# Gate matrices from two fp32r pieces, with one compare and one product for four tokens

## What is computed

```python
q = (t @ w_pq).reshape(T, PEER_HEADS, 2, PEER_HALF)
s = einsum('thpk,hpnk->thpn', q, sub_keys)
top_s, top_i = lax.top_k(s, PEER_TOPK)                       # 16 of 128 keys, twice per head
cand_s = top_s[:, :, 0, :, None] + top_s[:, :, 1, None, :]
best_s, best_pos = lax.top_k(cand_s.reshape(...), PEER_TOPK) # 16 of 256 pairs
gate = jax.nn.softmax(best_s, axis=-1)
act = gelu(einsum('td,thkd->thk', t, expert_down[experts]))
out = einsum('thk,thkd->td', gate * act, expert_up[experts])
```

## Time and profile before

| what | us |
|---|---|
| median of 3 runs | 3011.03 (3009.43 to 3012.24) |
| the profiled execution | 3016.37 |
| its span | 3014.6 |
| PE busy | 2911.4 |
| DVE busy | 2404.4 |
| ACT busy | 1478.6 |
| POOL busy | 691.7 |

### The profile page before, as it was taken

The page is one execution under the profiler, slowest core; times in us unless marked ns, Lnnn a source line. Parts: engine busy times, 40 slices in busy tenths (PEclk is TensorE's granted clock), DMA queues, the critical chain, the costliest instruction groups (busy, mean ns, idle before and its releaser), DMA issues. The chain is left out here.

```text
span 3014.6 us, 49268 instructions
## 1 busy us (share of the span) xinstructions
PE 2911.4 (97%) x19366; PEld 2671.4 (89%) x19366; DVE 2404.4 (80%) x4049; ACT 1478.6 (49%) x2443; POOL 691.7 (23%) x374
## 2 busy tenths in 40 slices
PE   7899999999999998999999999999899999999998
PEld 7798989879898987999999888888799999988887
DVE  5978998687899876898997677777599899656665
ACT  3453434445443444545665455554444666545554
POOL 0100000010000011797665000001289666300000
PEclk9999999999999998999999999999899999999999
DMA  6435555543555552454445777873245444555554
GB/s 221 154 138 204 198 200 190 199 168 133 187 198 209 189 193 92 170 182 156 141 141 189 242 262 260 290 272 118 105 166 184 141 140 141 175 182 194 191 195 161
DMA packets 125976, 547.96 MB, mean 182 GB/s; under 512 B 13715, under 2 KB 17972, under 8 KB 101300
## 3 DMA queue, kind: packets, MB, share of 16 engines
q1 hardware_dynamic: 124572, 542.73, 51.5%
q10 hardware_dynamic: 1176, 2.10, 0.4%
HBM read 538.48 MB, written 6.29 MB: 181 GB/s over the span
## 5 line engine op out<-in xcount | busy, mean ns | idle before, releaser
L2025 POOL TENSOR_TENSOR q_lo<-q_raw,q_hi 128x1024 fp32r<-128x1024 f32 x250 | 624.9, 2506 | 261.7 <-ACT q_hi L2135 261.4
L2044 PE MATMUL k_psN<-k_hhi,q_hi 128*128 128x256 f32 x2304 | 666.6, 289 | 0.7 <-ACT e_hv L2199 0.2
L2044 PE MATMUL k_psN<-k_hhi,q_lo 128*128 128x256 f32 x2304 | 652.9, 283 | 0.0
L2044 PE MATMUL k_psN<-k_hlo,q_hi 128*128 128x256 f32 x2304 | 652.7, 283 | 0.0
L2135 ACT ACTIVATE q_hi<-q_raw 128x1024 fp32r<-128x1024 f32 x538 | 565.3, 1051 | 6.6 <-DMA q_raw<-down 3.5
L2338 DVE TENSOR_TENSOR q_lo<-q_raw,q_hi 128x1024 fp32r<-128x1024 f32 x288 | 352.9, 1225 | 130.6 <-ACT q_hi L2135 130.0
L2044 PEld LDWEIGHTS k_psN<-k_hhi,q_hi 128*128 128x128 f32 x2304 | 443.0, 192 | 3.1 <-DVE k_hlo L2364 2.4
L2044 PEld LDWEIGHTS k_psN<-k_hlo,q_hi 128*128 128x128 f32 x2304 | 443.3, 192 | 0.0
L2044 PEld LDWEIGHTS k_psN<-k_hhi,q_lo 128*128 128x128 f32 x2304 | 442.4, 192 | 0.0
L752 DVE TENSOR_TENSOR k_wlo<-k_raw,k_whi 128x2048 fp32r<-128x2048 f32 x158 | 360.9, 2287 | 95.2 <-ACT k_whi L572 94.4
L572 ACT ACTIVATE k_whi<-k_raw 128x2048 fp32r<-128x2048 f32 x158 | 301.7, 1913 | 230.6 <-PE f_psA L424 99.6
(11 more groups left out here) (357 smaller groups left out, 5485.1 us busy)
## 6 DMA issues: line engine op xcount, KB each, us to landing
k_raw<-ws SPq DMA_DIRECT2D x180, 1024.0 KB, 4.8
q_raw<-down SPq DMA_DIRECT2D x288, 512.0 KB, 3.4
q_raw<-up SPq DMA_DIRECT2D x256, 512.0 KB, 4.0
k_x<-ada SPq DMA_DIRECT2D x48, 512.0 KB, 3.6
e_ada<-ada SPq DMA_DIRECT2D x48, 512.0 KB, 5.1
out<-k_x SPq DMA_DIRECT2D x3, 1024.0 KB, 3.9
k_x<-out SPq DMA_DIRECT2D x3, 1024.0 KB, 6.2
k_x<-x SPq DMA_DIRECT2D x2, 1024.0 KB, 6.0
```

The source lines that it names most:

```text
L2025: nc.gpsimd.tensor_tensor(lo[:, i % RING, :], raw[:, i % RING, :], hi[:, i % RING, :].bitcast(F32), ALU.subtract).then_inc(S["lo_pool"], 1)
L2044: last = nc.tensor.matmul(psD(n), w, h, start=kt == 0 and i == 0, stop=kt == KT - 1 and i == 2)
```

## The change

The gates are split into two fp32r pieces, `gT_hi` (rounded) and `gT_lo` (the difference). One DVE compare of 128x1024 for four tokens writes both one-hot matrices, for i1 and for i2 (`compared`). The rows of the first matrix are multiplied by the high piece in one 128x512 DVE product (`high_rows`), and by the low piece in four ScalarE activations of 128x128 with one scale per partition (`low_rows`). PE multiplies the one-hot matrix of i2 by both, in two fp32r matmuls per token, summed in PSUM. The buffers of a group are two deep instead of three, the ring B has 6 slots instead of 11. DVE's order in an iteration becomes `compared(g)`, `into_a(g-2)`, `high_rows(g)`, `gate_early(g-3)` (for g = 0 and 1 the high rows follow the compare at once). ScalarE's own rows, which needed no other engine, are gone; `low_rows` waits for the compare.

```diff
@@ -1857,10 +1857,10 @@
 ND = PQ + NE
 NU = ND + NE
 FIRST = 45
-SLOTS = 11
+SLOTS = 6
 GROUP = 4
 GROUPS = T // GROUP
-HOTS = 3
+HOTS = 2
 RING = 3
 
 INSIDE = GROUPS
@@ -1907,13 +1907,15 @@
     pb = arena(nc, env["X_at"], tag)
     B_at = pb.at[0]
     B = pb("e_b", [P, SLOTS, T])
-    i1T, i2T, gT = (pb("e_" + n, [P, T]) for n in ("i1T", "i2T", "gT"))
-    ngT = pb("e_ngT", [P, GROUPS])
+    iT = pb("e_iT", [P, 2, T])
+    gT_hi = pb("e_gThi", [P, T], F32R)
+    gT_lo = pb("e_gTlo", [P, T])
     iota = pb("e_iota", [P, P])
     hot_at = pb.at[0]
-    hot1 = pb("e_hot1", [P, HOTS, GROUP, NE])
-    hot2 = pb("e_hot2", [P, HOTS, GROUP, NE])
-    assert pb.at[0] == env["peer_at"]
+    hot = pb("e_hot", [P, HOTS, 2, GROUP, NE], F32R)
+    row_hi = pb("e_rhi", [P, HOTS, GROUP, NE], F32R)
+    row_lo = pb("e_rlo", [P, HOTS, GROUP, NE], F32R)
+    assert pb.at[0] <= env["peer_at"]
     raw, hi, lo = env["peer_ring"]
     A_at = pb.at[0] = env["ring_at"]
     A = pb("e_a", [P, NE, T])
@@ -1958,7 +1960,7 @@
         psN = env["psN"]
         ps = cx.enter_context(nc.psum_tensor("e_ps" + str(l), [P, 4, CH], F32))
         names = """in_const in_keys diag_ready half_done tile_diag hv_ready h_lo_ready norm_mm lo_pool lo_dve unit_done psd_read score_mm sc_copied
-            dve_step t_sub t_exp iv_ready picks_mm picks_copied hot1_ready hot2_ready hot1_act dist_ready neg_ready w_mm w_read_dve w_read_act
+            dve_step t_sub t_exp iv_ready picks_mm picks_copied hot_ready row_hi_ready row_lo_ready w_mm w_read_dve w_read_act
             weighted g_hi_ready g_lo_ready gate_mm gate_ready prod_done x_done out_x in_crow in_ada ada_done""".split()
         S = {n: cx.enter_context(nc.semaphore("e_" + n + str(l))) for n in names}
         raw_in = [Q["raw0"], Q["raw1"], Q["raw2"]]
@@ -2056,14 +2058,14 @@
 
                 def gates(g):
 
-                    pe.wait_ge(S["hot1_ready"], g + 1)
-                    pe.wait_ge(S["hot2_ready"], g + 1)
-                    pe.wait_ge(S["hot1_act"], g + 1)
+                    pe.wait_ge(S["row_hi_ready"], g + 1)
+                    pe.wait_ge(S["row_lo_ready"], g + 1)
                     if g >= 4:
                         pe.wait_ge(S["w_read_act"], g - 3)
                     for k in range(GROUP):
-                        last = nc.tensor.matmul(ps[:, g % 4, k * NE:(k + 1) * NE], hot2[:, g % HOTS, k, :], hot1[:, g % HOTS, k, :],
-                                                start=True, stop=True)
+                        for i, row in enumerate((row_hi, row_lo)):
+                            last = nc.tensor.matmul(ps[:, g % 4, k * NE:(k + 1) * NE], hot[:, g % HOTS, 1, k, :], row[:, g % HOTS, k, :],
+                                                    start=i == 0, stop=i == 1)
                     last.then_inc(S["w_mm"], 1)
 
                 def up(x):
@@ -2167,16 +2169,15 @@
                     act.wait_ge(S["score_mm"], h + 1)
                     nc.scalar.activation(sc[:, h, :, :].rearrange("p a n -> p (a n)"), psS(h), ACT.Copy).then_inc(S["sc_copied"], 1)
 
-                def gated_last(g):
-
-                    k = GROUP - 1
-                    t = g * GROUP + k
+                def low_rows(g):
+
                     if g >= HOTS:
                         act.wait_ge(S["w_mm"], g - HOTS + 1)
-                    row = hot1[:, g % HOTS, k, :]
-                    nc.scalar.activation(row, iota[:, :], ACT.Abs, bias=i1T[:, t:t + 1], scale=-1.0).then_inc(S["dist_ready"], 1)
-                    act.wait_ge(S["dist_ready"], g + 1)
-                    nc.scalar.activation(row, row, ACT.Relu, bias=gT[:, t:t + 1], scale=ngT[:, g:g + 1]).then_inc(S["hot1_act"], 1)
+                    act.wait_ge(S["hot_ready"], g + 1)
+                    for k in range(GROUP):
+                        t = g * GROUP + k
+                        ins = nc.scalar.activation(row_lo[:, g % HOTS, k, :], hot[:, g % HOTS, 0, k, :].bitcast(F32), ACT.Copy, scale=gT_lo[:, t:t + 1])
+                    ins.then_inc(S["row_lo_ready"], 1)
 
                 def to_a(g):
 
@@ -2207,17 +2208,15 @@
                         scores_out(n // 2 - 1)
                     head(n + RING)
                 act.wait_ge(S["picks_copied"], 3)
-                nc.scalar.activation(ngT[:, :], gT[:, :].rearrange("p (g k) -> p g k", k=GROUP)[:, :, GROUP - 1], ACT.Copy, scale=-1.0).then_inc(S["neg_ready"], 1)
-                act.wait_ge(S["neg_ready"], 1)
-                gated_last(0)
-                gated_last(1)
+                low_rows(0)
+                low_rows(1)
                 for g in range(GROUPS):
                     if g:
                         n = PQ + FIRST + g - 1
                         take(n)
                         head(n + RING)
                     if g + 2 < GROUPS:
-                        gated_last(g + 2)
+                        low_rows(g + 2)
                     to_a(g)
                 for n in range(PQ + FIRST + INSIDE - 1, ND):
                     take(n)
@@ -2303,18 +2302,19 @@
                     own.link(V.tensor_tensor(hots[:, :, :, :], hots[:, :, :, :], num, ALU.mult))
                     own.step(V.tensor_reduce(iv[:, 0:2, :, h * 16:(h + 1) * 16].rearrange("p k t s -> p (k t) s"), hots[:, :, :, :], AX.X, ALU.add))
 
-                def gated(g):
+                def compared(g):
 
                     if g >= HOTS:
                         dve.wait_ge(S["w_mm"], g - HOTS + 1)
-                    for k in range(GROUP - 1):
-                        t = g * GROUP + k
-                        ins = V.tensor_scalar(hot1[:, g % HOTS, k, :], iota[:, :], i1T[:, t:t + 1], gT[:, t:t + 1], ALU.is_equal, ALU.mult)
-                    ins.then_inc(S["hot1_ready"], 1)
-                    tokens = slice(g * GROUP, (g + 1) * GROUP)
-                    V.tensor_tensor(hot2[:, g % HOTS, :, :], iota[:, :].rearrange("p (a n) -> p a n", a=1).to_broadcast([P, GROUP, NE]),
-                                    i2T[:, tokens].rearrange("p (a n) -> p a n", n=1).to_broadcast([P, GROUP, NE]),
-                                    ALU.is_equal).then_inc(S["hot2_ready"], 1)
+                    numbers = iT[:, :, g * GROUP:(g + 1) * GROUP].rearrange("p a (k n) -> p a k n", n=1).to_broadcast([P, 2, GROUP, NE])
+                    places = iota[:, :].rearrange("p (a k n) -> p a k n", a=1, k=1).to_broadcast([P, 2, GROUP, NE])
+                    V.tensor_tensor(hot[:, g % HOTS, :, :, :], places, numbers, ALU.is_equal).then_inc(S["hot_ready"], 1)
+
+                def high_rows(g):
+
+                    dve.wait_ge(S["hot_ready"], g + 1)
+                    high = gT_hi[:, g * GROUP:(g + 1) * GROUP].bitcast(F32).rearrange("p (k n) -> p k n", n=1).to_broadcast([P, GROUP, NE])
+                    V.tensor_tensor(row_hi[:, g % HOTS, :, :], hot[:, g % HOTS, 0, :, :].bitcast(F32), high, ALU.mult).then_inc(S["row_hi_ready"], 1)
 
                 def into_a(g):
 
@@ -2375,18 +2375,25 @@
                 own.link(V.tensor_reduce(esum[:, :], e, AX.X, ALU.add))
                 own.link(V.reciprocal(esum[:, :], esum[:, :]))
                 V.tensor_tensor(e, e, esum[:, :].rearrange("p (a c) -> p a c", c=1).to_broadcast([P, 16, 16]), ALU.mult).then_inc(S["iv_ready"], 1)
-                for i, dst in enumerate((i1T, i2T, gT)):
-                    dve.wait_ge(S["picks_mm"], i + 1)
-                    V.tensor_copy(dst[:, :], ps[:, i, 0:T]).then_inc(S["picks_copied"], 1)
+                dve.wait_ge(S["picks_mm"], 2)
+                V.tensor_copy(iT[:, :, :], ps[:, 0:2, 0:T]).then_inc(S["picks_copied"], 1)
+                dve.wait_ge(S["picks_mm"], 3)
+                V.tensor_copy(gT_hi[:, :], ps[:, 2, 0:T]).then_inc(S["picks_copied"], 1)
+                dve.wait_ge(S["picks_copied"], 2)
+                V.tensor_tensor(gT_lo[:, :], ps[:, 2, 0:T], gT_hi[:, :].bitcast(F32), ALU.subtract).then_inc(S["picks_copied"], 1)
                 dve.wait_ge(S["picks_copied"], 3)
 
                 for g in range(GROUPS + 3):
                     if g < GROUPS:
-                        gated(g)
+                        compared(g)
+                        if g < HOTS:
+                            high_rows(g)
+                    if 2 <= g < GROUPS + 2:
+                        into_a(g - 2)
+                    if HOTS <= g < GROUPS:
+                        high_rows(g)
                     if g >= 3:
                         gate_early(g - 3)
-                    if 2 <= g < GROUPS + 2:
-                        into_a(g - 2)
                 for n in range(PQ + FIRST + INSIDE, ND):
                     weigh(n)
                     rest(n + RING)
```

## The result

| | before | after |
|---|---|---|
| median, us (4 runs each) | 3011.64 (3009.43 to 3012.44) | 3077.34 (3075.0 to 3080.63) |
| the profiled execution, us | 3016.37 | 3077.74 |
| its span, us | 3014.6 | 3076.0 |

The change makes the kernel slower: the ratio is 1.0219 with an interval of [1.0206, 1.0232]. That is 65.7 us between the medians and 61.4 us between the two profiled executions. Forecast was +54, 3065 us, with a range of 3038 to 3130.

The account below looks back on a forecast made before the run. PE bounds the kernel before; after the change DVE's and POOL's turns were to set the gate stage's pace. Turns 43, phase 14 and first gates -3 gave +54 us on 3011: 3065 us, range 3038 to 3130 us.

Parts of the forecast that it names:

- PE gains nothing: Gate products on PE: 8 fp32r records replace 8 at 0.112 to 0.120 us, losing at most 0.06 us a group.
- Rival 1: Gate products on PE: fp32r no cheaper than fp32 at 128 columns, 0.224 us each, 3121 us; chance 0.27.
- rival 3: Gate stage: DVE-POOL turns are no bound, PE decides; with records at 0.081 us, 2977 us; chance 0.09.
- The turn cycle of 4.02 to 4.27 us: Gate stage: DVE and POOL alternating take mean 4.15 us a group against PE's 3.77, 48 us in all.
- the lead: DVE starts each layer's gate stage 2.6 us ahead of PE; eating that up cuts the loss from 48 to 43 us.
- Rivals 3 and 4: Gate stage: turns are no bound; records cheaper than 0.112 us (chance 0.09), or at 0.112, 3008 to 3015 us (0.07).
- First gates -3 us: Start of the second layer's gates: two turns behind POOL replace four, shortening PE's wait by about 3 us.
- ScalarE and DMA hide: Gate stage: ScalarE's 2.7 us a group fits under 3.77 us; DMAs and their queue are untouched.
- The phase term of +14 us: Later 63 groups: in half, POOL precedes the compare and DVE's product into A lies bare, 32 x 0.45 us.
- A close finish goes to POOL: Gate stage: when a DVE compare and POOL's subtraction start nearly together, POOL gets its turn first.
- Rival 2: Gate stage: every POOL turn falls ahead of the compare, +97 us, 3108 us; chance 0.07.
- Fewer buffers are free but for the lead: Gate stage: two hot buffers only limit DVE's lead of 2.6 us; 6 slots of ring B cost nothing.

Follow-up runs that it names:

- E9: The changed kernel with DVE making POOL's low halves in the gate stage, each gate product cut into two of 64 columns: 3126.59 us.
- E3: The changed kernel with ScalarE's low rows of two tokens made in two halves each, six activations for four: 3056.84 us.
- E1: The changed kernel with POOL subtracting only the first 512 of 1024 columns for the gate stage's tiles: 3014.07 us.
- E2: The changed kernel with POOL's whole subtraction for the gate stage's tiles given to DVE: 3014.99 us.
- E12: The kernel before with a ring B of 6 slots in place of 11, keeping three hot buffers: 3012.28 us.
- E4: The changed kernel without the low piece of each fourth token, one activation and one gate product less per group: 3095.91 us.
- E11: The changed kernel with only DVE's new compare and product, in fp32, no low rows, three hot buffers, 5 slots of B: 3075.61 us.
- E7: The kernel before with the change's buffers alone, two hot buffers for three and 6 slots of B for 11: 3037.02 us.
- E6: The kernel before with POOL's subtraction for the gate stage's tiles given to DVE: 3009.72 us, ratio 0.9999.
- E8: The changed kernel with POOL's gate-stage subtraction on DVE, no low rows, and PE using the gates' high piece only: 2957.58 us.

## Why the prediction was right, and where it was off

Every step below is one of the prediction's own.

- **PE gains nothing: right.** Eight records at 0.112 us for eight. Rival 1 (0.224 us a record, 3121 us) falls by the rows at 1420 us, rival 3's cheaper record by the same rows and by E9. What the prediction held for rival 1, a fixed cost "that fp32 doesn't have", isn't in its rows: an fp32 record of 128 columns at 0.112 us is 0.059 us over 128 columns at 2.4 GHz (0.053 us), more than fp32r's 0.013.
- **The turn cycle of 4.02 to 4.27 us: right.** E3 shows it undisturbed, from 4.06 to 4.27, 4.22 in the mean of the last 25; the change has 4.04 in its first groups. The forecast sum of 43 us after the lead compares with E3's 41.6. That the price of one turn (3.35 us) was taken from another stage did no harm. Rivals 3 and 4, turns no bound, fall by E1 and E2.
- **First gates -3 us: not shown, the near match is luck.** In the two profiled executions the first gates come 1.3 and 1.5 us earlier, where 3 us were forecast for the second layer alone. But the wait of 4.44 us belongs to that one execution of before. E12, the kernel before with fewer slots of B and the same median, waits less:

```profile
2352.06 2.04 PE L2065 MATMUL e_ps<-e_hot,e_hot 128*128 128x128 f32 x8 [2.67 <-ACT e_hot L2179]
```

The changed kernel waits the same 2.67 us, for ScalarE's low rows. Against E12 its first gates are level in the first layer (1393.43 and 1393.45 us) and 0.8 us later in the second.
- **ScalarE and DMA hide: right as work, wrong as time.** ScalarE was never late for PE after the first group, but the moment at which it lets POOL go is worth 20 us either way (E3, E4).
- **The phase term of +14 us: the step that failed.** That the product into A lies bare once POOL comes ahead of the compare was right, the size not, and that POOL's turns would come in pairs was not foreseen. I put the release at 4.12 us, and it is 4.25 falling to 4.15; I priced a bare product at 0.45 us, and it is 4.68 - 4.22 = 0.46. What failed is the count: "half of the later 63 groups", 32. Once the crossing has come, every group to the end of the layer pays in the mean, 25 a layer, 50 in all: 23 us (22.4 by the whole stages). The groups there are 3.83 to 5.59 us apart, outside the 4.0 to 4.4 that the prediction named as its sign. "Half" was a guess where the numbers allowed a count, the cycle as it grows from group to group against the release.
- **A close finish goes to POOL: wrong as a rule.** At 1538.34 POOL is recorded 0.03 us ahead and the compare runs free; at 1546.68 it is 0.03 us ahead and the compare stands. The recorded starts don't tell who wins when they are 0.03 us apart. The Trainium skill (SBUF — State Buffer, "Who interferes with whom") lets whoever issues first hold the shared pair; starts this close, like those of the earlier trace rows, can neither confirm nor refute it.
- **Rival 2, every turn ahead of the compare (3108 us): not the change,** whose turns are behind it for 38 intervals. E4 comes near it with 3095.91 us, and its turns too come in pairs.
- **Fewer buffers are free but for the lead: right here, wrong in general.** For the changed order E11 bears it out in fp32 and without the low rows; with them no run has three hot buffers. For the old order two hot buffers cost 26 us (E7), with turns bunched in the same way, which I didn't see coming.
- **The carried offset.** The profiled execution of before lay 5.3 us over its median, that of after 0.4 us over. In profiled time I forecast 3070.4 and got 3077.74, off by 7.4: +8.4 for the phase, -1.4 for the turns, 0.4 for the rest. By the medians I am off by 12.3, and the other 4.9 us are this offset. It lies where the two layers' gates begin: E12's span is 5.8 us shorter than that of before, 1.3 and 2.3 us of it before the first gates and 1.5 and 0.7 in the first interval behind them. The prediction carried it over to a kernel that doesn't show it.

What stays open: no version was found that keeps both pieces of the gates and beats before; E1 leaves work out and E2 only draws level. The change with both pieces and three hot buffers was not run: by the sizes in the code they take more than the stage has for them. Why POOL's turns pair up, and stay paired, is read from timelines; no run changed that link alone. PE's 8 records and 24 matmuls hold the groups at 3.77 us with and without the change once POOL is out of the way (E2, E6), which makes a gain there unlikely unless products are left out, as in E8.

## What to carry to other kernels

When two engines take turns on something, count the turn-taking work of each per period (here 1.31 us became 1.94) and add the other's whole turn; if the sum passes the period of the engine that binds, the turns set the pace (here 4.0 to 4.3 us for 3.77), and fewer instructions don't help. Then compare the length of that cycle, group by group, with the delay at which the other engine is released: where they crossed here, overlap was lost until the end of the layer, and moving the release by 0.3 us, in one direction by adding work to ScalarE, was worth about 20 us either way. And before shortening a stall that the profile shows, ask whether anyone waits for it (E6: 25 us of DVE's time in a stretch of 230, nothing gained).

## What the runs showed of the hardware

- A gate product of 64 or 128 columns in fp32r costs 0.112 us in a stream (E9, the change), as does each of the two records of an fp32 product of 128 columns (before).
- DVE's compare of two repeated (broadcast) inputs, writing fp32r, takes turns with POOL as the product of the earlier trace rows does: 1.21 us free, 3.41 to 3.43 behind a subtraction.
- TensorE's granted clock fell after some of the new idle spells. In the changed kernel PE is idle for 1.44 us before the gate products of 1579.18, and in 1580.40 to 1583.40 the granted clock is 0.50, the lower level of 1.2 GHz; then it is back at 0.98. In this layer the clock fell twice in the late groups, at 1580 and 1618 us, for eleven idle spells of 0.98 us or more. No run shows what this cost.
